# Depthwise convolution in a conformer block: 31 taps split anew between TensorE and VectorE, and the layer norm's statistic taken another way

## The reference, cut to what matters

```
a, gate = split(x @ w_pw1 + b_pw1, 2)         # 1024 -> 2 x 1024
h = a * sigmoid(gate)
h = depthwise_conv(h, w_dw, width 31, padding 15 on both sides) + b_dw
y = (h - mean(h)) * rsqrt(mean((h - mean(h))**2) + 1e-5) * ln_g + ln_b
out = silu(y) @ w_pw2 + b_pw2                 # added to the residual stream
```

## Time and profile before

| | |
|---|---|
| time, median of 3 | 2888.2 us (2883.78 to 2891.26) |
| the profiled execution | 2889.76 us, of which its span 2888.1 us |
| PE, PEld busy | 94%, 76% of the span |
| DVE busy | 56% |
| ACT busy | 35% |
| POOL busy | 13% |
| mean granted PE clock | 0.96 of full |
| data moved by DMA | 227 MB, 79 GB/s |

### The profile page before, as it was taken

How to read it: one execution, slowest core, us unless ns; L and a number is a source line. 1 busy time by engine, 2 the same in 40 slices (tenths; PEclk the granted TensorE clock), 3 DMA queues, 4 the chain that set the end, 5 groups by cost and what they waited for, 6 DMA issues and landing times.

```text
span 2888.1 us, 38616 instructions
## 1 busy us (share of the span) xinstructions
PE 2708.9 (94%) x14597; PEld 2190.2 (76%) x14597; DVE 1623.4 (56%) x2360; ACT 1003.5 (35%) x1423; POOL 380.4 (13%) x277
## 2 busy tenths in 40 slices
PE   7899989878999989999999999999999896999998
PEld 5677767667677767888888888888888775788886
DVE  5556554644656565554454445554455897754445
ACT  4443434434665653222253222232222211422222
POOL 1100000000200002111121111121111242211110
PEclk9999999988999999999989999999999997999998
DMA  3221222102222221233212322323232210222321
GB/s 115 67 74 60 74 60 74 60 15 73 81 73 80 73 73 59 87 102 102 87 59 88 102 87 102 100 90 102 87 102 87 73 46 12 88 91 99 102 87 58
DMA packets 167800, 227.34 MB, mean 79 GB/s; under 512 B 5361, under 2 KB 148219, under 8 KB 167699
## 3 DMA queue, kind: packets, MB, share of 16 engines
q1 hardware_dynamic: 163523, 217.23, 22.8%
q0 software_dynamic: 2368, 8.47, 0.8%
q10 hardware_dynamic: 1808, 0.21, 0.0%
HBM read 223.71 MB, written 2.18 MB: 78 GB/s over the span
## 4 chain that ended last, share of the span: by engine, by line
PE 78%; DVE 11%; issue 6%; ACT 4%; DVEq 0%; POOL 0%; DMA 0%; ACTq 0%; SPq 0%; POOLq 0%
PE ps L376 19%; PE ps L378 19%; PE ps L377 19%; PE ps L761 3%; PE ps L763 3%; PE ps L762 3%; DVE w_lo L357 2%; DVE dw_y L2058 1%; DVE probs L1579 1%; PE ps L1449 1%; PE ps L366 1%; PE ps L367 1%; PE ps L368 1%; ACT w_hi L352 1%; PE ps L1460 1%
## 5 line engine op out<-in xcount | busy, mean ns | idle before, releaser
L352 ACT ACTIVATE w_hi<-w_raw 128x2048 fp32r<-128x2048 f32 x203 | 388.3, 1913 | 898.4 <-PE ps L378 895.3
L376 PE MATMUL ps<-h_hi,w_hi 128*128 128x512 f32 x1472 | 573.8, 390 | 4.8 <-DVE glu L2027 3.6
L378 PE MATMUL ps<-h_hi,w_lo 128*128 128x512 f32 x1472 | 572.8, 389 | 0.0
L377 PE MATMUL ps<-h_lo,w_hi 128*128 128x512 f32 x1472 | 572.7, 389 | 0.0
L357 DVE TENSOR_TENSOR w_lo<-w_raw,w_hi 128x2048 fp32r<-128x2048 f32 x203 | 471.9, 2324 | 131.3 <-ACT w_hi L352 131.3
L376 PE MATMUL ps<-a_hi,w_hi 128*128 128x512 f32 x1024 | 404.7, 395 | 33.8 <-issue 17.4
L421 DVE SCALAR_TENSOR_TENSOR xT<-ps,xT 128x512 f32<-128x512 f32 x504 | 336.2, 687 | 150.9 <-PE ps L378 150.0
L377 PE MATMUL ps<-a_lo,w_hi 128*128 128x512 f32 x1024 | 402.1, 393 | 0.0
L378 PE MATMUL ps<-a_hi,w_lo 128*128 128x512 f32 x1024 | 402.1, 393 | 0.0
L1663 POOL TENSOR_TENSOR f_gate<-f_gate,n_rstd 128x512 f32<-128x512 f32 x88 | 176.8, 2011 | 1123.5 <-ACT f_gate L1657 1123.5
L376 PEld LDWEIGHTS ps<-h_hi,w_hi 128*128 128x128 f32 x1472 | 276.3, 188 | 63.1 <-DVE glu L2027 4.5
(11 more groups left out here) (329 smaller groups left out, 3060.8 us busy)
## 6 DMA issues: line engine op xcount, KB each, us to landing
w_raw<-in_ffn_w_in_dram SPq DMA_DIRECT2D x88, 1024.0 KB, 5.0
w_raw<-in_ffn_w_out_dram SPq DMA_DIRECT2D x44, 1024.0 KB, 4.9
w_raw<-in_a_w_in_dram SPq DMA_DIRECT2D x24, 1024.0 KB, 5.3
w_raw<-in_b_w_in_dram SPq DMA_DIRECT2D x16, 1024.0 KB, 5.4
w_raw<-in_conv_w_pw_dram SPq DMA_DIRECT2D x12, 1024.0 KB, 5.3
w_raw<-in_a_w_out_dram SPq DMA_DIRECT2D x8, 1024.0 KB, 4.9
w_raw<-in_b_w_out_dram SPq DMA_DIRECT2D x8, 1024.0 KB, 5.0
bias_cur<-rel_scratch POOLq DMA_DIRECT2D x8, 512.0 KB, 3.8
```

Source lines behind the costliest of these rows:

```text
L352: nc.scalar.activation(w_hi[:, t % 2], w_raw[:, t % 2], ACT.Copy).then_inc(hi_done, 1)
L376: nc.tensor.matmul(dst, wh, xh, start=(k == 0), stop=False)
L377: nc.tensor.matmul(dst, wh, xl, start=False, stop=False)
L378: m = nc.tensor.matmul(dst, wl, xh, start=False, stop=last)
```

## The change

- **Taps.** 20 of the 31 taps go to PE and 11 stay on DVE (22 instructions a pair instead of 40). PE's product is now plain float32 with no hi and lo parts, so `glu_hi`, `glu_lo`, `taps_hi`, `taps_lo`, `diag_hi` and `diag_lo` are gone.
- **Blocks.** A group g of 32 channels is handled by itself. `shifted[32u.., c, g]` holds, on the 32 partitions of group u, the group's `glu` shifted by u columns (u = 0 to 3). One product of a 128x32 block (`tap_blocks`: four stacked 32x32 diagonals) with 512 columns then does four taps of 32 channels. Five such steps make 20 taps; they go around the four groups, whose outputs lie on different 32 partitions of a bank. That is 20 matmuls a chunk.
- **Copies by DMA.** The shifted copies are made by 16 DMAs a chunk, each of 32 partitions by 528 columns (67.6 KB), issued by ACT right behind the chunk's sigmoid (`act_shifted`), once `glu` of that chunk is written.
- **Taps over partitions.** `act_taps` issues 16 small DMAs ahead of the squares of norm 6, which spread the tap values in the same way. POOL builds one 128x640 block array per chunk in place of two arrays of 128x1408.
- **Order.** PE does the `a` tile, the taps of the last pair, then the `gate` tile; the first half of the `a` tile no longer waits for the second chunk's `glu`. DVE adds PE's sums before the next pair's `glu`, not after it. The last pair's taps go on PE behind the first six of the eight mean sums.
- **Layer norm.** The sum of squares is a product of ones with `n_sq` (512 columns), so that it stands on all partitions at once. ACT takes its logarithm and then exp(-0.5 · log) in 128x512, straight into `n_rstd`. The square root, the reciprocal, two copies and the way back over PE are gone for this norm.

```diff
-PE_TAPS = 11
+SHIFTS = 4
+PE_STEPS = 5
+PE_TAPS = SHIFTS * PE_STEPS
...
+            shifted = sb("shifted", [P, 2, 4, T + PE_TAPS - SHIFTS], into=s)
+            taps_x = sb("taps_x", [P, 4, PE_STEPS, KC], into=s)
+            tap_blocks = sb("tap_blocks", [P, 2, 4 * PE_STEPS, BK], into=s)
...
         def pe_taps(pe, i=None):
-            pe.wait_ge(glu_lo_done, KC // 2 if i is None else i + 1)
             pe.wait_ge(taps_added, KC if i is None else i * 2 + 2)
             for c in range(2):
...
+                pe.wait_ge(glu_moved[c], KC // 2 * GLU_MOVES if i is None else i * GLU_MOVES + GLU_MOVES)
+                for j in range(PE_STEPS):
+                    for g, r in enumerate(ROWS):
+                        ins = nc.tensor.matmul(ps[r, 4 + c], tap_blocks[:, c, g * PE_STEPS + j],
+                                               shifted[:, c, g, j * SHIFTS:j * SHIFTS + T], start=j == 0, stop=j == PE_STEPS - 1)
+                ins.then_inc(taps_done, 1)
...
             with pe.Fori(0, KC // 2 - 1) as i:
-                for k in range(NC):
-                    pe_tile(pe, T_PW1 + NC + k, i, NC, all_free=k == 0)
+                t = T_PW1 + NC
+                pe_tile(pe, t, i, NC, between=lambda: pe.wait_ge(in_free, at(in_before, t, i, NC) + IN_CREDIT))
                 pe_taps(pe, i)
-            pe_taps(pe)
+                pe_tile(pe, t + 1, i, NC)
             in_all_free(pe, T_PW2)
             for n in range(KC):
...
+                elif n == KC - 2:
+                    pe_taps(pe)
+                    pe.wait_ge(taps_added, KC + 2)
                 ins = nc.tensor.matmul(ps[:, 0], ones[:], dw_y[:, n], start=n == 0, stop=n == KC - 1)
...
                 pe.wait_ge(sq_ready, 8 * m + n + 1)
-                for c in range(TC):
-                    ins = nc.tensor.matmul(ps[:, 6, c:c + 1], n_sq[:, n % 2, c * P:c * P + P], ones[:, 0:1],
-                                           start=n == 0 and c == 0, stop=n == KC - 1 and c == TC - 1)
-                ins.then_inc(sum_ready if n < KC - 1 else stat_ready, 1)
-            pe_spread(pe, m)
+                nc.tensor.matmul(ps[:, 6], ones[:], n_sq[:, n % 2], start=n == 0, stop=n == KC - 1
+                                 ).then_inc(sum_ready if n < KC - 1 else stat_ready, 1)
...
+        def act_taps(act):
+            tap_rows = cols[:, PARAMS["dw"]:PARAMS["dw"] + PE_TAPS * KC].rearrange("p (j u n) -> p u j n", u=SHIFTS, n=KC)
+            for u, to in enumerate(ROWS):
+                for g, r in enumerate(ROWS):
+                    act.dma_start(taps_x[to, g], tap_rows[r, u]).then_inc(taps_moved, 16)
+
+        def act_shifted(act, base, c, i=None):
+            n = base + c
+            act.wait_ge(in_free, at(in_before, T_PW1 + base, i, NC) + (2 * c + 2 + IN_CREDIT))
+            act.wait_ge(taps_done, n + 1 if i is None else i * 2 + (n + 1))
+            for u, to in enumerate(ROWS):
+                for g, r in enumerate(ROWS):
+                    src = glu[r, n:n + 1] if i is None else glu[r, bass.ds(i * 2 + n, 1)]
+                    act.dma_start(shifted[to, c, g], src[:, :, u:u + T + PE_TAPS - SHIFTS].rearrange("p o t -> p (o t)")
+                                  ).then_inc(glu_moved[c], 16)
...
                 nc.scalar.activation(glu_s[:, c], ps[:, 2 + c], ACT.Sigmoid, bias=bias).then_inc(glu_act, 1)
-        def act_glu_hi(act, i=None):
...
+                act_shifted(act, base, c, i)
...
-            act_root(act, m, 3)
+            act.wait_ge(stat_ready, m + 1)
+            nc.scalar.activation(n_rb[:], ps[:, 6], ACT.Ln, bias=eps[:, 3:4], scale=1.0 / D).then_inc(ln_logs, 1)
+            act.wait_ge(ln_logs, 1)
+            nc.scalar.activation(n_rstd[:], n_rb[:], ACT.Exp, scale=-0.5).then_inc(ln_rstd, 1)
...
-            v.tensor_tensor(glu_lo[:], g, glu_hi[:].bitcast(F32), ALU.subtract).then_inc(glu_lo_done, 1)
...
                 dve_taps(dve, i, T_PW1 + NC + 1)
+                dve_taps_add(dve, i)
                 dve_glu(dve, NC, i)
-                dve_taps_add(dve, i)
...
-            dve_rstd(dve, m, copied=True)
+            dve.wait_ge(ln_rstd, 1)
...
             act_ff(act, 2, 5)
+            act_taps(act)
             act_squares(act, 6, added(end_of(2)))
```

More of the change, by code:

```diff
@@ L318, in build @@
         POOL_STAT = 3
-        COPIED = (1, 2, 4, 5, 7, 8, 9)
+        COPIED = (1, 2, 4, 5, 8, 9)
+        ROOTED = [m for m in range(10) if m != LN_STAT]
         SCALED = (0, 1, 2, 7)
-        SPREAD = [m for m in range(10) if m != POOL_STAT]
+        SPREAD = [m for m in range(10) if m not in (POOL_STAT, LN_STAT)]
         junk_ready = sem("junk_ready")
@@ L490, in dve_inverse @@
         def dve_inverse(dve, m):
-            dve.wait_ge(root_ready, m + 1)
+            dve.wait_ge(root_ready, ROOTED.index(m) + 1)
             if m:
@@ L497, in dve_widen @@
             dve_inverse(dve, m)
-            dve.wait_ge(inv_ready, m + 1)
+            dve.wait_ge(inv_ready, ROOTED.index(m) + 1)
             nc.vector.tensor_copy(n_rb[:].rearrange("p (c q) -> p c q", q=P),
@@ L508, in dve_rstd @@
         def dve_rstd(dve, m, copied=False, meanwhile=None):
[L509 to L512, removed]
+            dve.wait_ge(sq_ready, 8 * m + 8)
+            dve.wait_ge(sum_ready, 7 * m + 7)
+            nc.vector.tensor_tensor(n_sum[:], n_sum[:], n_sq[:, (KC - 1) % 2], ALU.add).then_inc(total_ready, 1)
             if m in FIRST_TILE:
@@ L1907, in build @@
         taps_done, diag_ready = sem("taps_done"), sem("diag_ready")
-        glu_hi_done, glu_lo_done, taps_split = sem("glu_hi_done"), sem("glu_lo_done"), sem("taps_split")
         taps_added = sem("taps_added")
+        taps_moved, ln_logs, ln_rstd = sem("taps_moved"), sem("ln_logs"), sem("ln_rstd")
+        glu_moved = [sem("glu_moved0"), sem("glu_moved1")]
         DW_STEPS = 2 * (DW - PE_TAPS)
-        tap_rows = cols[:, PARAMS["dw"]:PARAMS["dw"] + PE_TAPS * KC]
+        GLU_MOVES = 16 * 4 * SHIFTS
         ln_pe = Marks(sem("ln_pe"), ["sum"])
@@ L1916, in pe_taps @@
         def pe_taps(pe, i=None):
-            pe.wait_ge(glu_lo_done, KC // 2 if i is None else i + 1)
             pe.wait_ge(taps_added, KC if i is None else i * 2 + 2)
             for c in range(2):
-                pe.wait_ge(diag_ready, 4 * (KC // 2) - 2 + 2 * c if i is None else i * 4 + (2 + 2 * c))
-                products(ps[:, 4 + c], [(diag_hi[:, c, j], diag_lo[:, c, j], glu_hi[:, c, j:j + T],
-                                         glu_lo[:, c, j:j + T]) for j in range(PE_TAPS)]).then_inc(taps_done, 1)
+                pe.wait_ge(diag_ready, KC - 1 + c if i is None else i * 2 + (1 + c))
+                pe.wait_ge(glu_moved[c], KC // 2 * GLU_MOVES if i is None else i * GLU_MOVES + GLU_MOVES)
[4 more added lines that the diff above has]
+                ins.then_inc(taps_done, 1)
         def pe_conv(pe, m, q):
@@ L1950, in gp_taps @@
         def gp_taps(pool):
-            pool.wait_ge(taps_split, 2)
+            pool.wait_ge(taps_moved, 16 * 4 * SHIFTS)
             with pool.Fori(0, KC // 2) as i:
@@ L1955, in gp_taps @@
                     pool.wait_ge(taps_done, i * 2 + (1 + c))
[L1956 to L1959, removed]
+                    tap = (taps_x[:, :, :, bass.ds(i * 2 + c, 1)].rearrange("p g j o -> p (g j) o")
+                           .to_broadcast([P, 4 * PE_STEPS, BK]))
+                    nc.gpsimd.tensor_tensor(tap_blocks[:, c], block_mask[:, LEVELS:LEVELS + 1].to_broadcast([P, 4 * PE_STEPS, BK]),
+                                            tap, ALU.mult).then_inc(diag_ready, 1)
+        def act_taps(act):
[12 more added lines that the diff above has]
+                                  ).then_inc(glu_moved[c], 16)
         def act_glu(act, base, i=None):
@@ L2034, in dve_taps @@
             v = nc.vector
-            dve.wait_ge(glu_hi_done, KC // 2 + 1 if i is None else i + 2)
-            g = glu[:, KC - 2:KC] if i is None else glu[:, bass.ds(i * 2, 2)]
-            v.tensor_tensor(glu_lo[:], g, glu_hi[:].bitcast(F32), ALU.subtract).then_inc(glu_lo_done, 1)
             if t is not None:
                 split_tile(dve, t, i, NC)
+            dve.wait_ge(in_free, in_before(T_PW2) + IN_CREDIT if i is None else at(in_before, T_PW1 + NC, i, NC) + IN_CREDIT)
             def pc(r):
```

23 lines of the change are left out of this document (3 added, 20 removed).

## The result

The changed kernel takes **2900.6 us** (median of 8 runs, 2897.2 to 2905.4); the kernel before, run beside it on the same chip, takes 2885.3 (2882.8 to 2891.3). The ratio is **1.005, 95% interval 1.004 to 1.006**: slower by 15 us. The forecast was 2872, 17 less than the execution it was worked from, and 2900.6 lies above the range.

The account below looks back on a forecast made before the run. The convolution stage was taken as bound by DVE, with a tail behind it. Taps' issues 4.6, cycles -3.7, tail -12.8 and layer norm -5.1 sum to -17.0 us, giving 2872 us, range 2852 to 2898.

Parts of the forecast that it names:

- x: Time of one DMA issue on ACT: 0.36 us outside the loop, 0.47 in it, bounds 0.29 and 0.60.
- The formula around x: Convolution cycle, glu 0 to next glu 0, through ACT and DVE: 25.8 + 32x, so 37.3 us first, then 40.8 twice.
- rival C: Issues are dear: 128 us more per us of x; at 0.20 more, 2898 us, slower by 10; chance 0.27.
- Its own chain: The convolution cycle's chain through ACT and DVE, in which DVE was said to stand idle about 9.5 us a cycle.
- Rival D: PE's column groups don't run side by side with 128 rows: 17.2 us a chunk, 2946 us or so; chance 0.08.
- `act_taps`: Ahead of norm 6's squares: 16 DMA issues at 0.40 us, 6.4 in all, costing 4.6 us on the path.
- Cycles: Three convolution cycles, 37.3 us then 40.8 twice, against 39.9, 41.5 and 41.2 before: 3.7 us less.
- Tail: From the end of the last pair's glu 0 to the end of the mean sums: 28.2 us instead of 41.0, 12.8 less.
- Layer norm: From the end of the mean sums to the first silu: 13.2 us instead of 18.3, 5.1 less.
- PE's taps: 40 records a chunk on PE take 4.3 us with all four column groups side by side; bounds 4.3 and 17.2.
- Landing: Time for the shifted copies to land after issue: 2.5 us, taken from 2.7 for 512 KB.
- Rival B: Issues cost 0.1 us or less, PE sets a 30.5 us cycle: 2834 us; chance 0.10 for all below 2863.

Follow-up runs that it names:

- price kernel: The changed kernel plus 24 extra DMAs of different shapes on SP, then the same 24 on ACT, to read issue times; 2913.2 us in one run, not compared.
- split tail: Against the kernel with everything on SP: the last chunk's 16 copies issued by ACT beside SP's 16 of the chunk before; 2847.2 us, ratio 0.986.
- the kernel with everything on SP: The changed kernel with all 144 DMAs (taps and shifted copies) issued by SP between its reordered weight loads; 2852.5 us, ratio 0.990.
- The way through DRAM: Against the kernel with everything on SP: each chunk goes to DRAM in one DMA and returns in four, 5 issues instead of 16; 2833.9 us, ratio 0.982.

## Why the prediction was wrong

**The step that failed** is "I take x = 0.36 us outside the loop (nearer to SP's, since SP is quiet here) and x = 0.47 in it. Bounds 0.29 and 0.60". An issue took 0.67 in both places, above the upper bound. Two faults lie in it. First, every row behind it was a transfer from DRAM, and the new ones go from SBUF to SBUF. The price kernel shows 0.17 us between the two as the length of a record, on both engines; ACT's DRAM-sourced ones lay 0.53 apart in the earlier trace rows, which should have been the value; even so, 0.53 throughout would have given 2884, so the greater part is the SBUF source, for which I had no row. Second, I counted SP's being quiet as a discount and let SP's 0.29 pull the value down, though that row stands beside one of ACT's (6.64 and 6.75 us) and is of 0.2 KB transfers. In the price kernel SP and ACT issue at different times and pay the same, and in the split tail they issue at once and pay the same.

**The formula around x held.** It said 25.8 + 32x for a cycle, through ACT and DVE in the order told. Taking out of the three cycles the 21.3, 21.5 and 21.3 us of issues leaves 25.2, 25.7 and 26.0. With x = 0.67 and 0.69 for the taps, the sum is 2872 + 16·0.29 + 32·0.31 + 80·0.20 = 2872 + 4.6 + 9.9 + 16.0 = 2902.5; measured 2900.6. So rival C is what happened, with its own slope of 128 us for each us of x. I gave it 0.27 but only 0.07 of that to the slower side, because I let x rise by no more than 0.20 over a value that was already low.

Three smaller slips in the working change nothing above. Its own chain leaves DVE idle twice a cycle, by some 8.7 and 9.4 us, and not 9.5 in all (measured 11.2 and 13.0 in the first). The layer norm's terms add up to 13.1, not 13.2. Rival D's add up to 2948, not 2946.

**Term by term:**

- `act_taps`: forecast 4.6, measured 5.8 in the profiles and 7.0 by moving it. It is the same price again, 16 at 0.69 instead of 0.40. The last norm sum ends 7.5 us late (its start is 2252.63 instead of 2242.38, less the 2.8 from ahead), and 1.7 of that is won back before glu 0.
- Cycles: forecast 3.7 less, measured 18.4 more.
- Tail: from the end of glu 0 forecast 28.2, measured 32.6. 3.3 of the 4.4 are chunk 0's 16 issues (glu 1 ends at 12.5 instead of 9.2), 0.8 PE's wait for chunk 1's landing. The first six mean sums took 7.5, as forecast. PE had been idle for 19.8 us; its granted clock was 0.50, the lower level, for the first 4.1 us of the sums and full from then on.
- Layer norm: forecast 5.1 less, measured 5.0 in the stage and 5.3 alone.
- PE's taps: 40 records a chunk took 4.50 us with the last record's own length, so all four column groups ran at once (one by one they would take 17.3) and rival D fell. By the Trainium skill (TensorE: Matmul & The Clock Gate, Packing small matmuls) three column tiles give 2.38 times; here four gave the full four, so the measured row decides for the shorter time.
- Landing: 2.0 us, forecast 2.5.

**Rival B's rule.** The Trainium skill (DMA: Bandwidth & Descriptors, Anatomy of one DMA) puts a sequencer's dispatch at about 50 ns, as one part of a transfer on GpSimd's path; the transfers here are issued by SP and ACT. The shortest issue of the copies, in any of these kernels, is 0.30 us, and those of this change held their sequencer for 0.67, so the measured rows decide against taking the page's figure as the price of an issue here.

**What the prediction didn't see** is how near the change was to a large gain. Rival B had its size, but only for cheap issues, at a chance of 0.10; fewer issues weren't thought of. The relief of DVE brought the stage to PE's pace, 30.7 us a cycle, as soon as the issues were out of ACT's way. The kernel needed 16 issues a chunk because each DMA moves one block of 32 rows; with the regrouping in DRAM it needs five. Not tried: fewer PE taps at that pace, the taps' own 16 issues through DRAM, and merging a pair's returns.

## What to carry to other kernels

Issuing a DMA is an instruction of the engine that issues it, so count issues and multiply by a row of the same kind (the same memories at both ends, and a similar shape), and see what stands behind them in that engine's order. An engine with low busy time may still be the one that everybody waits for; look at its queue rows and at the "issue" releasers. When the slope of a term is as steep as 128 us for a us, the range has to follow the term's worst row, and the count is worth lowering before the price is known.

## What the runs showed of the hardware that was not expected

- The length of an issue differed with the memories at both ends. It was 0.34 us for SBUF to DRAM (128 rows, 271 KB), 0.42 to 0.45 for the copies and for 32 x 528 from DRAM to SBUF, and 0.54 to 0.61 at the median for SBUF to SBUF, where sizes from one row of 528 to 128 rows of 528 made no difference. With the gap to the next one the last is 0.64 to 0.69. From DRAM to SBUF the shape or size counted too: SP took 0.37 for a weight tile of 1 MB and 0.25 for 0.2 KB.
- In the price kernel the length changes one issue late. The first DRAM-sourced one behind those from SBUF took 0.60 us on ACT and 0.58 on SP, and the first from SBUF behind the four from DRAM 0.53 and 0.51. Why is open.
- With the counter in the address the record was shorter (0.54 instead of 0.61) and a register operation of 0.046 us stood ahead of each, so the loop cost nothing extra:

```profile
L1979 ACTq DMA_DIRECT2D shifted<-glu x128: 535/536/1364, 2280.4 to 2444.5; - x128
L1979 ACTq FUSED_REGOPS  x96: 46/46/65, 2326.9 to 2444.4; - x96
```

- The way through DRAM moves 271 + 4 · 264 = 1327 KB a chunk instead of 16 · 66 = 1056 (not twice as much, as my second theory had it), and lands it in 2.9 + 6.1 us at the median instead of 2.0, and was still the fastest version.
- DVE's first eight taps took 5.38 us with none of POOL's builds of 128x640 among them (the kernel with everything on SP), 6.43 with one and 7.49 with two, so a build that falls on a tap costs DVE 1.05 us.
